# Passage between the two halves of a fused FFN: where the last activation pair is staged, which queue loads the first chunk, and when the residual's second half is loaded

## The reference, cut to what matters

```
u2 = _rmsnorm(h, ln2_g[i])
a, bb = jnp.split(u2 @ w_gate_upffn[i], 2, axis=-1)
h = h + (jax.nn.silu(a) * bb) @ w_down[i]
```

## Time and profile before

| | |
|---|---|
| median of three runs | 1751.95 us (1751.86 to 1752.31) |
| the profiled execution: its own time | 1748.73 us |
| the profiled execution: its span | 1746.9 us |
| PE busy | 1651.7 us (95% of the span) |
| PEld busy | 1361.6 us (78%) |
| DVE busy | 1166.8 us (67%) |
| POOL busy | 717.1 us (41%) |
| ACT busy | 621.5 us (36%) |
| mean granted PE clock | 0.981 |

### The profile page before, as it was taken

The page is one execution under the profiler, slowest core; times in us unless marked ns, Lnnn a source line. Parts: engine busy times, 40 slices in busy tenths (PEclk is TensorE's granted clock), DMA queues, the critical chain, the costliest instruction groups (busy, mean ns, idle before and its releaser), DMA issues.

```text
span 1746.9 us, 21566 instructions
## 1 busy us (share of the span) xinstructions
PE 1651.7 (95%) x7804; PEld 1361.6 (78%) x7804; DVE 1166.8 (67%) x1695; ACT 621.5 (36%) x973; POOL 717.1 (41%) x385
## 2 busy tenths in 40 slices
PE   6999999999989999999998899999889999979996
PEld 4888787887868888888876788877668888879775
DVE  7231799963497777776757566878847982485457
ACT  4031334421255444444433222254551111167214
POOL 4534211144414332332227587743255554442451
PEclk9999999999999999999998999999999999989998
DMA  4511010132513434434477966042001111200012
GB/s 172 87 46 49 25 37 25 37 115 91 216 70 136 157 133 160 153 149 165 157 277 281 385 273 245 26 155 59 26 24 48 48 45 40 85 1 1 24 37 97
DMA packets 52420, 190.22 MB, mean 109 GB/s; under 512 B 5681, under 2 KB 7618, under 8 KB 51562
## 3 DMA queue, kind: packets, MB, share of 16 engines
q1 hardware_dynamic: 49522, 179.47, 28.5%
q10 hardware_dynamic: 2808, 9.57, 2.2%
HBM read 133.97 MB, written 55.05 MB: 108 GB/s over the span
## 4 chain that ended last, share of the span: by engine, by line
PE 55%; DVE 8%; issue 3%; DMA 3%; ACT 2%; POOL 1%; POOLq 0%; DVEq 0%; ACTq 0%
PE G L710 15%; PE U L923 11%; PE G L923 10%; PE G L961 5%; PE U L961 5%; PE G L997 2%; PE U L1172 2%; DMA hid_spill<-hst 2%; PE G L1159 1%; PE U L1040 1%; PE G L1077 1%; DVE h L2128 1%; DVE B_lo L1763 0%; DVE hst L2064 0%; DMA h<-h_spill 0%
## 5 line engine op out<-in xcount | busy, mean ns | idle before, releaser
L566 POOL TENSOR_SCALAR w_hi<-raw 128x1024 fp32r<-128x1024 f32 x53 | 159.7, 3013 | 297.0 <-PE G L710 236.1
L710 PE MATMUL G<-A_hi,w_hi 128*128 128x512 f32 x464 | 151.8, 409 | 14.4 <-DVE A_lo L1765 11.6
L710 PE MATMUL G<-B_hi,w_hi 128*128 128x512 f32 x512 | 159.9, 393 | 4.6 <-DVE B_lo L1763 2.3
L710 PE MATMUL G<-B_lo,w_hi 128*128 128x512 f32 x512 | 157.8, 389 | 0.0
L710 PE MATMUL G<-B_hi,w_lo 128*128 128x512 f32 x512 | 157.7, 389 | 0.0
L710 PE MATMUL G<-A_lo,w_hi 128*128 128x512 f32 x464 | 145.7, 396 | 0.0
L710 PE MATMUL G<-A_hi,w_lo 128*128 128x512 f32 x464 | 144.5, 393 | 0.0
L568 POOL TENSOR_TENSOR w_lo<-raw,w_hi 128x1024 fp32r<-128x1024 f32 x53 | 142.3, 2685 | 4.4
L606 POOL TENSOR_TENSOR S<-fraw 128x512 f32<-128x512 f32 x33 | 46.0, 1395 | 217.0 <-DVE ring_lo L2025 200.4
L923 PE MATMUL U<-X_hi,ring_hi 128*128 128x512 f32 x308 | 122.2, 397 | 9.5 <-DVE ring_lo L2025 9.4
L1374 ACT ACTIVATE ring_hi<-S 128x512 fp32r<-128x512 f32 x132 | 82.1, 628 | 115.1 <-PE U L961 76.2
(11 more groups left out here) (355 smaller groups left out, 3797.1 us busy)
## 6 DMA issues: line engine op xcount, KB each, us to landing
hid_spill<-hst SPq DMA_DIRECT2D x77, 512.0 KB, 2.6
raw<-in_weights SPq DMA_DIRECT2D x73, 512.0 KB, 3.7
Dc<-hid_spill SPq DMA_DIRECT2D x70, 512.0 KB, 8.6
fraw<-in_weights SPq DMA_DIRECT2D x66, 512.0 KB, 4.5
h<-in_x_t SPq DMA_DIRECT2D x8, 512.0 KB, 7.8
h<-in_x_t ACTq DMA_DIRECT2D x1, 4096.0 KB, 13.7
h_spill<-h SPq DMA_DIRECT2D x8, 512.0 KB, 6.9
pj_spill<-pj_out SPq DMA_DIRECT2D x8, 512.0 KB, 3.5
```

The lines of the kernel that those rows point to most:

```text
L566: pool.tensor_scalar(hi, raw[:, u, :], 1.0, None, ALU.mult).then_inc(w_hi_done, 1)
L710: mm = pe.matmul(G[g][:, b * HT:(b + 1) * HT], w, x[:, k, b * HT:(b + 1) * HT], start=s0, stop=s1)
```

## The change

Five things change, all between the last up steps and down step 25:

1. Tiles q = 72 to 76 get buffers of their own (`hst_last`), so with the two of `hst` the last pair has seven. Their stores count on a semaphore of their own (`hs_last`). `hidden_hi` of these tiles waits for the last up product instead of a landed store, because four of the buffers lie over up operands (the fifth lies over `acc`).
2. Chunk 0 is loaded from ACT's queue, 14 DMAs between ACT's instructions of the last up steps, where SP issued them before.
3. On ACT all seven `hidden_hi` of the last pair stand ahead of `weights_hi(23, ...)`; before, five of them alternated with it.
4. On the DVE `hidden_lo` of tiles 72 and 73 and the last `turn_h` stand ahead of the first `down_add`; the other three follow the first three pairs of adds.
5. On SP the seven stores of a pair follow each other, `h_in(1)` waits for tiles 0 to 71 alone and is issued right after store 76, `raw_in(24)` follows it, and chunk 1 is loaded after that (its pieces 5 and 6 after the last stores have landed, over whose buffers they lie).

```diff
+        hst_last = [at(f"hst_last{j}", kb, [P, 2, HT], F32R) for j, kb in enumerate((96, 100, 104, 108, 196))]
...
+        def piece_of_pair(q):
+
+            own = q - NR * (GROUPS - 1) - 2
+            return hst[:, q % 2, :, :] if own < 0 else hst_last[own][:, :, :]
...
             raw_in(UP)
             last = NR * (GROUPS - 2)
-            hidden_out(last), hidden_out(last + 1)
-            chunks_in(0, UP - 1, 0, 1, 2, 3)
-            hidden_out(last + 2), hidden_out(last + 3)
-            chunks_in(0, UP - 1, 4, 5, 6)
-            for j in range(4, NR):
+            for j in range(NR):
                 hidden_out(last + j)
             raw_in(UP + 1)
...
             last += NR
-            hidden_out(last), hidden_out(last + 1)
+            for j in range(NR):
+                hidden_out(last + j)
+            for u in range(2):
+                sp.wait_ge(hs_out[u], 16 * (last // 2 + 1))
+            h_in(1)
             raw_in(UP + 2)
-            hidden_out(last + 2), hidden_out(last + 3)
-            for j in range(4, NR):
-                chunks_in(1, UP - 1, j - 4)
-                hidden_out(last + j)
-            landed(GROUPS)
-            h_in(1)
-            chunks_in(1, UP - 1, 3, 4, 5, 6)
+            chunks_in(1, UP - 1, 0, 1, 2, 3, 4)
+            sp.wait_ge(hs_last, 16 * len(hst_last))
+            chunks_in(1, UP - 1, 5, 6)
             raw_in(UP + 3)
...
-                if q >= 2:
+                if q >= NR * (GROUPS - 1) + 2:
+                    act.wait_ge(f_used[1], used(UP - 1, NR - 1))
+                elif q >= 2:
                     act.wait_ge(hs_out[q % 2], 16 * (q // 2))
...
+            def first_chunk_in(r):
+
+
+                for n in range(2):
+                    act.dma_start(f(Dc[0][:, r, n, :, :].rearrange("p a n -> p (a n)")), hid_spill[n, :, r, :]).then_inc(ch_in[0][r], 16)
...
                 if k in hi_at:
                     hidden_hi(NR * (GROUPS - 2) + hi_at[k])
+                if x and r < 4:
+                    first_chunk_in(2 * r)
+                    if r < 3:
+                        first_chunk_in(2 * r + 1)
...
-            hidden_hi(last), hidden_hi(last + 1)
+            for j in range(NR):
+                hidden_hi(last + j)
             for w in range(UP, LAST):
                 for r in range(NR):
                     weights_hi(w + 1, r)
-                    if w == UP and r < 5:
-                        hidden_hi(last + 2 + r)
...
             turn_h(last, 0), hidden_lo(NR * last), turn_h(last, 1), hidden_lo(NR * last + 1), turn_h(last, 2)
+            hidden_lo(NR * last + 2), hidden_lo(NR * last + 3), turn_h(last, 3)
             dve.wait_ge(h_back[0], 16)
             for r in range(NR):
                 down_add(r, 0, UP, 0, 0)
-                if r < 5:
-                    hidden_lo(NR * last + 2 + r)
-                if r == 2:
-                    turn_h(last, 3)
+                if r < 3:
+                    hidden_lo(NR * last + 4 + r)
```

More of the change, by code:

```diff
@@ L352, in build @@
         hs_out = [sem(f"hs_out{u}") for u in range(2)]
+        hs_last = sem("hs_last")
         ch_in = [tile_in[0:NR], [sem(f"ch_in1_{r}") for r in range(NR)]]
@@ L462, in hidden_out @@
             def hidden_out(q):
+                landed_in = hs_out[q % 2] if q < NR * (GROUPS - 1) + 2 else hs_last
                 sp.wait_ge(hl_done, q + 1)
[L464 to L468, removed]
+                sp.dma_start(hid_spill[q // NR, :, q % NR, :], f(piece_of_pair(q).rearrange("p a n -> p (a n)"))).then_inc(landed_in, 16)
             def chunk_in(c, r):
@@ L1414, in hidden_hi @@
                     act.wait_ge(ht_done, 4 * g + (None, None, 1, 2, 3, None, 4)[j])
-                if q >= 2:
+                if q >= NR * (GROUPS - 1) + 2:
+                    act.wait_ge(f_used[1], used(UP - 1, NR - 1))
+                elif q >= 2:
                     act.wait_ge(hs_out[q % 2], 16 * (q // 2))
-                act.activation(hst[:, q % 2, 0, :], h_src[j], ACT.Copy).then_inc(hh_done, 1)
+                act.activation(piece_of_pair(q)[:, 0, :], h_src[j], ACT.Copy).then_inc(hh_done, 1)
             projected_p(0), projected_p(1)
@@ L2063, in hidden_lo @@
                 dve.wait_ge(hh_done, q + 1)
-                dve.tensor_tensor(hst[:, q % 2, 1, :], h_src[q % NR], f(hst[:, q % 2, 0, :]), ALU.subtract).then_inc(hl_done, 1)
+                hi, lo = (piece_of_pair(q)[:, e, :] for e in range(2))
+                dve.tensor_tensor(lo, h_src[q % NR], f(hi), ALU.subtract).then_inc(hl_done, 1)
             inverse_q(2)
@@ L2141, in _ @@
                 if w == LAST:
+                    dve.wait_ge(hs_last, 16 * len(hst_last))
                     clear(acc[:, :])
```

## The result

| | before | changed |
|---|---|---|
| median of four runs | 1751.9 us (1749.93 to 1752.31) | 1736.05 us (1735.35 to 1737.84) |
| ratio of the two | | 0.9915, interval 0.9901 to 0.9929 |
| the profiled execution: time, span | 1748.73, 1746.9 us | 1736.2, 1734.4 us |

A forecast was written before the change was run, and what follows sets the result against it. PE, nearly always busy, was idle four times between the end of up and step 24. The sum 10.9 + 1.7 = 12.6 us gave 1736.1 us profiled (from 1748.73), 1739.4 median (from 1751.95); range 1735.5 to 1747.

The forecast's parts named there:

- Part 1: End of up: 14 chunk loads added to ACT at 0.66 us each start product (21,2) late, 1.3 us lost.
- Part 2: End of up: stores land in about 5 us, the wait at (21,6) goes, up ends 4.3 us earlier.
- a rival in which stores land no sooner: End of up: stores still take 10.05 us, 4.5 us less gain, 1743.9 us; chance 0.10.
- Part 3: DVE between up and down: eight instructions take 10.3 us before the first add; PE waits 5.4 us at (22,4), not 2.3.
- the clock falls once, 1.7 us, as before: Behind PE's wait at (22,4): one fall to the lower clock, costing 1.7 us.
- The 0.5 us for (22,5) and (22,6): First down products: 0.5 us allowed for adds with a hidden tile between them, where 3.49 us and a slow clock stood.
- none slow, 7 us better: Bound at (22,4): with none of the eight DVE instructions slow, PE's wait ends near nothing, 7 us better.
- Part 4: Residual's second half: issued near 942, landed by 951, so PE starts (23,4) at 957.4 without its wait or slow clock.
- Part 5: SP's queue afterwards: step 26's weights land at 993.2 to 998.6; up to 1.4 us lost at the slow end.

The follow-up runs named there:

- after_chunk_on_sp: The changed kernel with chunk 0's loads back on SP's queue between the stores: 1740.72 us, ratio 0.9939 to the kernel before.
- pool_after_turn: The changed kernel with POOL's sums for step 23 held back until the last `turn_h` has ended: 1736.11 us, ratio 0.99 to the kernel before.
- adds_first: The changed kernel with the DVE's order of before, first adds ahead of two `hidden_lo` and the last `turn_h`: 1741.75 us, ratio 0.993.
- split_half_adds: `pool_split` with the DVE's first nine adds ordered by which half of the load has landed: 1736.56 us, ratio 0.9913 to the kernel before.
- the best version: `split_half_adds` with step 24's weights issued behind the second store of the last pair: 1734.05 us, ratio 0.99 to the kernel before.
- pool_split: `pool_after_turn` with the residual's first half loaded in two DMAs of 1 MB, a semaphore each: 1735.22 us, ratio 0.9903 to the kernel before.
- issues_doubled: The changed kernel with chunk 0's 14 loads on ACT cut into 28 of half the size: 1743.28 us, ratio 0.9953 to the kernel before.
- after_h_late: The changed kernel with `h_in(1)` issued only after all stores landed, behind one weight load and three pieces of chunk 1: 1746.13 us, ratio 0.9968.
- only_act_queue: The kernel before with chunk 0 loaded from ACT's queue and nothing else changed: 1746.09 us, ratio 0.9972.
- adds_first_raw_early: `adds_first` with step 24's weights issued behind the second store of the last pair: 1738.74 us, ratio 0.9927 to the kernel before.

## Why the prediction came out right, and where its terms were off

The forecast for a profiled execution was 1736.1 us and it was 1736.2; for the passage 12.6 us less, and it was 12.9. The median came out at 1736.05, 3.3 us under the 1739.4 forecast. That rest isn't a term of the sum: I took the passage's 12.6 us off a median that was 3.2 us above the profiled execution of before, and the changed kernel's profiled execution lies at its median (1736.2, 1736.05). Why the profile of before was short isn't settled; the start of the passage alone moves by up to 3.9 us between traces. That the forecast and the profiled execution agree to 0.1 us is luck in part: two of the terms were wrong by 1.3 us each, in opposite directions.

*Part 1, issues on ACT: 1.3 us forecast, none measured.* (21,2) starts without a wait. ACT's timeline of the changed kernel shows what I had wrong:

```profile
890.52 0.62 ACT L1375 ACTIVATE ring_hi<-fraw 128x512 fp32r<-128x512 f32 x1
890.98 2.00 ACTq L1450 DMA_DIRECT2D Dc<-hid_spill  x2
893.08 0.63 ACT L1375 ACTIVATE ring_hi<-fraw 128x512 fp32r<-128x512 f32 x1 [1.94 <-PE U L924]
893.19 0.51 ACTq L1450 DMA_DIRECT2D Dc<-hid_spill  x1
893.62 0.62 ACT L1420 ACTIVATE hst<-T1h 128x512 fp32r<-128x512 f32 x1
893.72 1.64 ACTq L1450 DMA_DIRECT2D Dc<-hid_spill  x3
895.47 0.60 ACT L1402 ACTIVATE sf<-G 128x512 f32<-128x512 f32 x1 [1.23 <-PE G L924]
```

The first two of the eight issues ran before all this, from 890.11, while ACT still worked on a copy, and others run while the rounding or the hidden tile is under way: the issue at 893.19 starts 0.1 us after the rounding at 893.08 did and ends together with it. I had put issues and instructions end to end, behind the rounding. They overlap, and the copy `sf<-G` is released by PE, at 895.47 - 1.3 = 894.17, the time of the earlier trace rows. The price of an issue was right: the eight took 5.04 us, 0.63 each. They just fit: the first four end at 892.98 and hold the rounding to 893.08, 0.3 us later than before, and the last ends at 895.36, 0.1 us ahead of the copy. With 28 issues the copy was held and PE waited. The 14 issues were 326 to 1496 ns each, 491 in the middle:

```profile
L1450 ACTq DMA_DIRECT2D Dc<-hid_spill x14: 326/491/1496, 890.1 to 907.7; - x14
```

*Part 2, stores: the mechanism right, the size off.* The store of tile 65 landed in 6.9 us, not 5 (10.05 before), and the worst of all 77 in 7.6, not 10.0:

```profile
897.94 6.91 DMA hid_spill<-hst
```

It was still in time, because it was issued 2.0 us sooner than I had it (897.94 - 1.3 = 896.6, forecast 898.6), as nothing was lost in part 1: it landed at 903.5, where the forecast had 903.6. The store of tile 67 was issued at 905.0, as forecast, and landed 7.6 us later, not 5. So ACT's wait for it did not disappear, as I had written: it shrank from 6.67 to 4.10 us and ended at 912.7 instead of 916.84. That was soon enough for the weights behind it, and the wait at (21,6) went. That the queue is the cause is shown by `after_chunk_on_sp`, where the worst store takes 10.0 us again, while it is 7.5 to 8.6 in all kernels with the loads in ACT's queue. (22,0) starts 5.5 us earlier beside (20,0), not 4.3: the difference is part 1's. By the Trainium skill's rule that DMAs of different engines interleave on the same engines ("DMA: Bandwidth & Descriptors", "Issuing engines are not separate DMA queues") I had a rival in which stores land no sooner; the rows of the two kernels speak against it. By the Trainium skill, the same page, "Queues, rings and completion order", each DMA engine takes turns between the queues, by which a store lands sooner than behind the loads but later than alone; 6.91 us, between 2.6 and 10.05, agrees. The part's own worth is smaller than its 5.5 us, as `after_chunk_on_sp` shows: of these 1.6 remained in the passage (4 by the ratios).

*Part 3, the DVE: right, but the clock's term was too small.* The DVE's timeline of the changed kernel:

```profile
925.50 1.68 DVE L2071 TENSOR_TENSOR T1h<-cb 128x512 f32<-128x512 f32 x1
...
932.18 1.74 DVE L2071 TENSOR_TENSOR T2h<-cb,T1h 128x512 f32<-128x512 f32 x1
933.85 0.68 DVE L2077 TENSOR_TENSOR hst_last<-T1h,hst_last 128x512 fp32r<-128x512 f32 x1
...
935.65 0.67 DVE L2141 TENSOR_TENSOR h<-h,G 128x512 f32<-128x512 f32 x1
```

On the clock of before `turn_h` ran at 924.2 and the first add at 934.4, each 1.0 to 1.1 us sooner than forecast (925.2 and 935.5), because part 1 lost nothing. What lies between is as forecast: five instructions slow and three fast, 10.15 us for the eight (10.3), and PE's wait 5.57 us (5.4), since PE came sooner as well. POOL's last sum beside them starts at 931.85, its next instruction after a wait for ACT:

```profile
931.85 1.52 POOL L615 TENSOR_TENSOR S<-fraw,S 128x512 f32<-128x512 f32 x1
936.99 3.48 POOL L623 TENSOR_TENSOR ring_lo<-fraw,ring_hi 128x512 fp32r<-128x512 f32 x2 [3.61 <-ACT ring_hi L1375]
```

That POOL is the cause was argued in the prediction and is shown by `pool_after_turn`. The term that failed is "the clock falls once, 1.7 us, as before": it cost 3.0 us, and 3.0 again in the rerun. The granted clock over 10 us around the last wait of before and around this one, before and changed:

```profile
966.00:976.00 10.00, 7.65 (x27) 6.18 (x28) 8.49 (x15) 0.94 (x2) 1.29 (x1) 0.83 1.00 404
934.00:944.00 10.00, 7.53 (x21) 6.00 (x22) 10.00 (x17) 4.45 (x8) 7.01 (x5) 0.66 0.89 339
```

The missing 0.17 of 10 us are 3.4 us at half the clock, the missing 0.34 are 6.8 us. So the clock fell once, as forecast, but stayed down twice as long as after each wait before; all but 0.7 us of it PE was at work. The 0.5 us for (22,5) and (22,6) weren't needed. Together: 1.3 us from part 1 and the 0.5 saved, 1.3 lost to the clock and 0.2 to the longer wait, which leaves 0.3, and that is 12.9 against 12.6. My bound "none slow, 7 us better" was too good as well: with POOL away, the first half of the residual is the next to be late, and the passage gained 0.6 us.

*Part 4, the residual: right.* The load was issued at 941.57 - 1.3 = 940.3 (forecast near 942) and its first add ran at 948.4 (landed by 951); (23,4) started at 958.55 - 1.3 = 957.3 (957.4, where the errors of parts 1 and 3 cancel), and the clock stayed full behind it. Undone, it cost 7.0 us.

```profile
941.57 0.38 SPq L481 DMA_DIRECT2D h<-h_spill  x1
```

*Part 5, late next: right.* POOL started on step 26's weights at 996.20, 994.9 on the clock of before, in the forecast's 993.2 to 998.6, after 6.52 us of waiting for them, and PE waited nowhere in steps 24 to 32:

```profile
975.68 1.29 POOL L607 TENSOR_TENSOR S<-fraw 128x512 f32<-128x512 f32 x1 [6.93 <-DMA fraw<-in_weights]
...
996.20 1.29 POOL L607 TENSOR_TENSOR S<-fraw 128x512 f32<-128x512 f32 x1 [6.52 <-DMA fraw<-in_weights]
```

That this queue is the next bound is shown from two sides. Delayed by the DVE's order it cost PE 2.61 us (`adds_first`), and where all else is early it cost 1.81 us (`split_half_adds`); one weight load moved ahead of the last stores took the second away, and of the first all but 0.76 us, though 1.11 us came up at (26,0).

## What to carry to other kernels

Ask of a stall that is removed how much of it arrives: here the up end came 5.5 us sooner, and 1.6 us of it were left at the end of the passage (4 by the ratios), because the next wait was set by an engine that had more work in front of it than before. The order in one queue decides which of several waits lasts; a load whose user comes late, as the weights of step 24 behind the stores, can be the one that bounds the next version. And where several short waits can take the place of a long one, that can be worth more than their sum shows, since the clock stayed up after waits of up to 1.5 us in the best version. It isn't sure: after waits of 1.19, 1.07 and 1.84 us close together it fell all the same (`pool_split`).

## What the runs showed of the hardware

- Issuing a DMA cost ACT 0.33 to 1.50 us whether it moved 512 or 256 KB (14 issues with a median of 0.49, 28 with a median of 0.46), and the issues ran while earlier instructions of ACT were still being worked on. In the changed kernel ACT's list has them in groups of four, four, four and two. The first group held the next instruction by 0.3 us and the second by nothing; behind the third ACT was idle for 1.54 us, without harm to PE. In `issues_doubled` eight in a row left ACT idle for 4.19, 3.63 and 3.38 us.
- A store of 512 KB took 2.6 us in the median, 10.05 at most in the queue that held eight chunk loads ahead of it, and 7.5 to 8.6 at most, by kernel, when these loads were in ACT's queue.
- What a wait costs through the lower clock isn't one figure, and the wait's length alone doesn't set it. Behind the two waits of 5.57 us (the changed kernel, twice) the products lost 3.0 us, behind one of 5.51 in `after_h_late` 2.3, of 5.88 in `issues_doubled` 1.9 and 5.66 in `only_act_queue` 2.1; behind 4.75 in `after_h_late` 2.9 and 3.77 in `adds_first` 3.1; behind 3.03 in `after_chunk_on_sp` 1.6. All of these but the last had the lower clock for 6.8 us, part of it while PE still waited (0.7 us in the changed kernel, 3.3 in `issues_doubled`), where it costs nothing; the last, the four waits of before and the 3.64 us of `pool_after_turn` had it for 3.4 us. Waits of the same length differ: behind 3.75 us in `only_act_queue` it lasted 3.4 us, and behind 3.01 us in that kernel also 3.4, while behind 3.01 in `adds_first_raw_early` the granted clock stayed at 1.00. Why isn't settled by these runs.
- A DVE instruction of 128x512 on two float32 operands, neither of them in a bank of the matmuls, took 1.7 us beside POOL's sums and 0.68 without them, and adds with one operand from a matmul's bank took 0.67 in both (`pool_after_turn`, at 938.72 beside POOL's sum at 938.39).
